# Mixture-of-experts stage of a two-block model: experts in fixed order, rows of each split by bits into 128-, 64- and 32-row blocks

## Chip, cores and metric

The kernel runs on one core of a Trainium2 chip. The metric is the device time of one execution in microseconds (us). Everything is float32. The names of the engines are PE (TensorE), DVE (VectorE), ACT (ScalarE), POOL (GpSimd) and SP (SyncE, which only queues DMAs here).

## What is computed

Two transformer-like blocks over 1,024 tokens of width 1,024. The change lies in the feed-forward part of the first, a mixture of 32 experts: a token picks one of 4 groups, and in it the two best of 8 experts. Cut to that:

```python
p_group, g_idx = lax.top_k(group_probs, 1)
p_exp, e_local = lax.top_k(jax.nn.softmax(e_logits, axis=-1), TOP_K)      # TOP_K = 2, 8 experts of the group
gate = p_group * p_exp / jnp.sum(p_exp, axis=-1, keepdims=True)
flat_e = (g_idx * EXPERTS_PER_GROUP + e_local).reshape(-1)                # 2,048 pairs of token and expert
order = jnp.argsort(flat_e); tok = order // TOP_K
xs = xf[tok]                                                              # rows of 1,024
hid = silu(ragged_dot(xs, w1, group_sizes)) * ragged_dot(xs, w3, group_sizes)   # w1, w3: 1024 x 512 each
ys = ragged_dot(hid, w2, group_sizes) * gate[...]                         # w2: 512 x 1024
```

The sizes of the groups are known only on the chip; the instructions are fixed before. For the inputs used here the router sends to experts 0 to 31, in this order, 84, 29, 15, 50, 38, 32, 32, 28, 126, 111, 72, 24, 72, 92, 57, 100, 54, 96, 89, 14, 25, 23, 37, 18, 132, 213, 64, 47, 28, 40, 63 and 143 rows.

## The kernel before

The program is written out by hand, engine by engine, with semaphores. The stages follow one another: first projections, retention, a delta rule, the residual (which writes the normalised rows `xn_rows`), `route` (the router), `experts_pass`, then `mix` (which gathers each token's two result rows from `y_rows`) and the second block.

**Router.** `route_tensor` (L2095) and `route_vector` (L2140) find each token's experts, its rank among the rows of the expert, and from that its place in `y_rows`. `route_blocks_vector` (L2223) turns the 32 counts into a list of blocks: an expert's rows fill blocks of 128 as long as more than 64 are left; what is then left, 64 at most, is a half block. It writes to the table `experts` which expert each block has, how many blocks of each kind are used, and whether a block's expert differs from that of the block before. `route_places_vector` (L2276) makes the places, 16 small matmuls (L2121) the tokens of each block (`tokens`).

**Experts.** `experts_units` (L2323) fixes an order of 47 units, of which the used ones run: a full block (one expert, 128 rows), or a pair of half blocks (two experts, 64 rows each). Here 13 full blocks and 11 pairs are used, so 24 units run. In `experts_tensor` (L2561), `work` does on PE for a unit: 32 matmuls of 256 columns for w1 and w3, with the transposed rows `e_xsT` as the stationary operand, transposes of the gated result `e_hid` and of the next unit's rows, and 8 matmuls of 512 columns with w2. For a pair, `experts_matmul` (L2551) issues each of these twice, into two column halves of the array. The helpers of ACT (L2645) and DVE (L2696) do silu, gate, copies and the affine step on the way out of the transposes. Every unit ends with one store of 128 rows to `y_rows` from ACT's queue (L2670).

**Control.** Each engine reads three numbers from `experts` into registers (`used_blocks`, L2384) and then meets two branches at a unit (`experts_blocks`, L2535), which always lead straight on as long as units are used; after the last one it jumps over the rest.

**Weights.** An expert's three matrices are 6.3 MB. There are three sets of buffers. The first load is that of expert 0 from a fixed address, queued at the end of the residual (L2354). All others (`experts_load`, L2439) wait until the router's table is there, read the expert's number into a register, and load from an address made of it; a load is left out if the set already holds the expert. That makes 34 loads of an expert here: 12 for full blocks and 22 for half blocks. POOL gathers the rows of each unit six units ahead (L2493).

Of the kernel before, what the change touches and what calls it, by code (L numbers as in the profile page):

```python
# [10 lines left out]
F32 = mybir.dt.float32  # L11
# [23 lines left out]
FULLS = 2 * T // (P // 2 + 1)  # L35
BLOCKS = FULLS + NE // 2
# [1123 lines left out]
def delta_conv_signals(k):  # L1160

    return k.on(CONV_SIGNALS, "w_0 w_1 w_ab_loaded taps_loaded a_log_loaded dt_loaded dn_norm_loaded bias_got bias_stored rpb_spread y_cleared", way="_conv")
# [25 lines left out]
def delta_conv(k, s, b, hT, dtok, z, d, rpb_rows, bias_rows, zero, y_rows, ahead):  # L1188

    cleared = y_rows.rearrange("(p b) (n r c) -> n p (b r) c", p=P, n=CLEARINGS, c=P)  # L1190
# [3 lines left out]
    for p in range(1, CONV_PAIRS):  # L1194
        if p >= 2:
            k.nc.sync.wait_ge(*s.w_summed(4 * (p - 1)))
            k.nc.sync.wait_ge(*conv_made(s, p - 2, 6))
            for role in range(4):
                k.nc.sync.wait_ge(*channels_got(s, p - 2))
                channels_load(k, s, b, p, role)  # L1200
        for n in {1: (0,), CONV_PAIRS - 1: (7,)}.get(p, (2 * p - 3, 2 * p - 2)):
            k.nc.sync.dma_start(cleared[n], wide(zero[:, :], 1, BLOCKS * D // P // CLEARINGS)).then_inc(*s.y_cleared.up().inc)
# [3 lines left out]
    k.nc.sync.wait_ge(*s.y_cleared(CLEARINGS))  # L1206
# [680 lines left out]
def residual_signals(k):  # L1887

    return k.on("out_made rows_gated x_added squared eps_added rstd xn_ready turned_0 turned_1 half_0_out half_1_out",
                "w_got_0 w_got_1 x_got_0 x_got_1 x_got_2 x_got_3 x_stored xn_stored_0 xn_stored_1 first_set_got", way="_res")  # L1890
# [11 lines left out]
def residual(k, s, b, retT, deltaT, hT, affine, x_out, xn_out, route_s, route_w, sets):  # L1902

    residual_sync(k, s, b, x_out, xn_out, route_s, route_w, sets)
# [8 lines left out]
def residual_kept(s):  # L1913

    return s.x_stored, s.xn_stored_0, s.xn_stored_1, s.first_set_got


def residual_sync(k, s, b, x_out, xn_out, route_s, route_w, sets):

    sy = k.nc.sync  # L1920
    for n, got in enumerate((s.x_got_0, s.x_got_1, s.x_got_2, s.x_got_3)):
        for m in (2 * n, 2 * n + 1):
            sy.dma_start(b.x[m][:, :], k.io["x"][m * P:(m + 1) * P, :]).then_inc(*got.up().inc)
    route_load(k, route_s, route_w)
# [5 lines left out]
    for j in range(3):  # L1930
        experts_first_load(k, s, sets, j)
# [96 lines left out]
Route = namedtuple("Route", "wr br lg eq gp top ix ixf sel hot both a1 a2 a3 earlier cnt low left upto0 upto1 first lines whole blk ef place w2 row_of blk_of parts hp hb pos lT fresh below")  # L2028
# [7 lines left out]
def route_loads(k):  # L2036

    return k.on("", "w_group_loaded w_expert_loaded b_group_loaded b_expert_loaded", way="_route"), \
        RouteWeights(k.at("route_w", front_at(82), P, NK, NL), k.at("route_b", front_at(84), P, NL))
# [11 lines left out]
def route(k, loads, weights, h2T, gates, where, tokens, experts):  # L2051


    early, late, wait = packed(k, "route", N_AT), packed(k, "route", N_AT + 144 * KB), packed(k, "route", A_AT)
    b = Route(weights.w, weights.b, early("logits", NT, NL), early("eq", NT, NE), early("gp", NT, 8), early("top", NT, 8), early("ix", NT, 8, dt=U32),
              early("ixf", NT, 8), early("sel", NT, PER_GROUP), late("hot", 2, NT, NE), early("both", NT, NE), late("a1", NT), late("a2", NT), late("a3", NT),
              early("earlier", NT + 1, NE), early("cnt", NE, NT), early("low", NE), early("left", NE), early("upto0", 2, NE + 16), early("upto1", 2, NE + 16),
              late("first", 2, NE), late("lines", 2, NE), late("whole", NE), early("blk", FULLS + NE, NE), early("ef", FULLS + NE), late("place", NT, NE),
              late("w2", NT, NE), late("row_of", NT, 2), late("blk_of", NT, 2), late("parts", 2, NT, 2, dt=U32), wait("hp", NT, 2, P), wait("hb", NT, 2, BLOCKS),
              late("pos", NT, 2), early("lT", BANK), early("fresh", SAME - 1), late("below", NT))  # L2060
    s = k.on("columns_made columns_out logits_made group_shifted group_exp ratio_ready ratio_exp chosen_ready ranks_made counts_ready counts_laid places_ready places_read")
# [33 lines left out]
def route_tensor(k, s, b, h2T):  # L2095
# [17 lines left out]
    keep_warm(k, 4, 7)  # L2113
    pe.wait_ge(*s.counts_ready(1))
    pe.matmul(k.bank[5][:, 0:FULLS + NE], k.c("ones"), b.ef[:, :], start=True, stop=True).then_inc(*s.counts_laid.up().inc)
    keep_warm(k, 7, 7)
    for n in range(NT):
        for j in range(2):
            if n % 4 == j == 0:
                pe.wait_ge(*s.places_ready(n // 4 + 1))  # L2120
            t = pe.matmul(k.bank[3][:, 0:BLOCKS], b.hp[:, n, j, :], b.hb[:, n, j, :], start=n + j == 0, stop=n + j == NT)  # L2121
# [18 lines left out]
def route_vector(k, s, loads, b, gates, where, tokens, experts):  # L2140
# [3 lines left out]
    v.tensor_scalar(b.below[:, :], k.c("token"), -float(NO_TOKEN), None, ALU.add).then_inc(*V.up().inc)  # L2144
    route_groups_vector(k, s, loads, b)
# [18 lines left out]
    v.wait_ge(*s.ratio_exp(1))  # L2164
    v.scalar_tensor_tensor(a3, a2, 1.0, a1, ALU.add, ALU.mult).then_inc(*V.up().inc)
    v.wait_ge(*V.now())
    v.reciprocal(gates[:, :, 0:1].squeeze(2), a3).then_inc(*V.up().inc)
    v.wait_ge(*V.now())
    v.tensor_tensor(gates[:, :, 1:2].squeeze(2), gates[:, :, 0:1].squeeze(2), a2, ALU.mult).then_inc(*V.up().inc)
# [9 lines left out]
    known = route_blocks_vector(k, s, b, experts)  # L2179
# [1907 lines left out]
```

## Time and profile before

| | |
|---|---|
| median of 3 runs | 3054.93 us |
| lowest and highest | 3054.62 and 3062.04 us |
| span of the profiled execution | 3061.1 us |
| own time of the profiled execution | not listed; the highest of the three runs is 0.9 us above the span |
| PE busy | 94% of the span |
| experts' stage, first to last matmul | 953.9 to 1516.8 us of the span |

The profile's page lists busy time of each engine and the costliest groups of instructions; the trace behind it can be asked for stretches, for one engine's instructions in order of time, and for the DMA queues. "Issue" names idle time in which an engine waited for nothing that the trace shows; a wait for a DMA's semaphore that stands in a separate instruction is such a case. A matmul of f32 is recorded as two passes, and a weight load (PEld) before each.

### The profile page before, as it was taken

The page shows a single profiled execution, that of the slowest core. Times are in us where ns is not written, and L with a number is a line of the kernel's source. Part 1 is how long each engine was busy: PE and PEld are TensorE (multiplying, and loading weights), DVE is VectorE, ACT ScalarE, POOL GpSimd, SP SyncE. Part 2 cuts the span into 40 slices and gives each one's busy share as a digit, 9 for nine tenths or more (in the row PEclk, how much of TensorE's full clock was granted, in tenths as well). Part 3 has the DMA queues.
Part 4 walks back from the last instruction along what each step waited for, and adds up shares of the span by engine and source line. Part 5 has one row for each costly group of instructions (what it writes and reads, how often), then busy time and mean ns, then how long its engine had stood idle before and what let it go on. Part 6 is the DMA issues. An engine that isn't in the chain of part 4 may idle for free.

```text
span 3061.1 us, 30798 instructions
## 1 busy us (share of the span) xinstructions
PE 2887.6 (94%) x12002; PEld 1715.2 (56%) x12002; DVE 1208.1 (39%) x1999; ACT 629.8 (21%) x1351; POOL 724.5 (24%) x552
## 2 busy tenths in 40 slices
PE   7999998888988999899889999999999999999998
PEld 5886544888446666566534455557544444444443
DVE  6714776565132111111143135479643314133142
ACT  4001232232121222212222211147230000000001
POOL 3213466543111000000021000146521122111220
PEclk9999999999998999999989999999999999999999
DMA  8734495000237999999661100030201101111101
GB/s 264 224 54 49 99 221 142 1 29 29 112 138 285 396 425 427 425 426 394 252 226 55 55 0 15 14 107 1 90 28 55 55 28 41 41 55 46 37 28 55
DMA packets 180120, 415.12 MB, mean 136 GB/s; under 512 B 30644, under 2 KB 103796, under 8 KB 170872
## 3 DMA queue, kind: packets, MB, share of 16 engines
q1 hardware_dynamic: 163545, 370.52, 34.2%
q10 hardware_dynamic: 10512, 25.69, 2.6%
q0 software_dynamic: 5904, 16.78, 1.5%
q8 instruction: 100, 1.64, 0.2%
q14 instruction: 59, 0.48, 0.0%
HBM read 372.33 MB, written 59.88 MB: 141 GB/s over the span
## 4 chain that ended last, share of the span: by engine, by line
PE 86%; DVE 6%; DMA 3%; issue 2%; ACT 1%; POOL 1%; SPq 0%; ACTq 0%; POOLq 0%; DVEq 0%
PE bank L3791 27%; PE bank L2554 9%; PE bank L2557 8%; PE bank L2984 5%; PE bank L1266 4%; PE bank L748 4%; PE bank L1946 4%; PE bank L3158 3%; PE bank L232 3%; PE bank L3156 2%; PE bank L3490 2%; PE bank L883 2%; PE bank L3500 2%; PE bank L1844 1%; DMA wa_rest<-in_w_ada 1%
## 5 line engine op out<-in xcount | busy, mean ns | idle before, releaser
L3791 PE MATMUL bank<-w_ff,uT 128*128 128x512 f32 x640 | 276.0, 592 | 0.0
L3791 PE MATMUL bank<-hT,w_ff 128*128 128x512 f32 x512 | 224.3, 596 | 4.3 <-DVE hT L3594 4.3
L3914 DVE TENSOR_TENSOR x_out<-x_out,bank 128x512 f32<-128x512 f32 x140 | 94.5, 685 | 291.8 <-PE bank L3791 291.6
L3791 PEld LDWEIGHTS bank<-w_ff,uT 128*128 128x128 f32 x640 | 121.6, 190 | 153.1 <-issue 153.1
L2554 PE MATMUL bank<-e_w,e_xsT 128*128 128x256 f32 x832 | 186.0, 385 | 1.6 <-DVE e_xsT L2640 1.6
L2554 PEld LDWEIGHTS bank<-e_w,e_xsT 128*128 128x128 f32 x832 | 159.3, 193 | 33.0 <-issue 11.3
L2557 PE MATMUL bank<-e_w,e_xsT 128*64 128x256 f32 x1408 | 155.9, 380 | 22.3 <-issue 22.3
L2984 PE MATMUL bank<-w_gla,nT 128*128 128x512 f32 x384 | 168.3, 598 | 2.0 <-ACT nT L2946 1.3
L3791 PEld LDWEIGHTS bank<-hT,w_ff 128*128 128x128 f32 x512 | 97.5, 191 | 126.3 <-issue 126.1
L3791 PE MATMUL bank<-h_sum,w_ff 128*128 128x512 f32 x384 | 166.1, 592 | 0.0
L2711 DVE TENSOR_TENSOR e_hid<-e_act,bank 128x256 f32<-128x256 f32 x48 | 20.2, 422 | 338.4 <-PE bank L2554 172.1
L2557 PEld LDWEIGHTS bank<-e_w,e_xsT 128*64 128x64 f32 x1408 | 111.6, 137 | 70.4 <-issue 33.9
L3855 POOL TENSOR_TENSOR w_ff<-w_ff,w_ff 128x2048 f32<-128x2048 f32 x9 | 42.7, 4746 | 355.8 <-PE bank L3791 352.5
L2984 PEld LDWEIGHTS bank<-w_gla,nT 128*128 128x128 f32 x384 | 73.2, 192 | 92.5 <-issue 89.1
L3828 ACT ACTIVATE uT<-bank 128x512 f32<-128x512 f32 x48 | 28.3, 600 | 468.9 <-PE bank L3791 468.9
L3791 PEld LDWEIGHTS bank<-h_sum,w_ff 128*128 128x128 f32 x384 | 73.0, 190 | 91.8 <-issue 91.8
L3901 DVE TENSOR_TENSOR uT<-uT,bank 128x512 f32<-128x512 f32 x48 | 32.9, 686 | 229.2 <-PE bank L3791 229.2
L3158 PE MATMUL bank<-nT,w_nqk 128*128 128x512 f32 x256 | 121.7, 605 | 0.0
L2493 POOL DMA_INDIRECT e_rows<-xn_rows,e_idx x25 | 25.0, 1001 | 407.8 <-PE bank L2523 379.8
L748 PE MATMUL bank<-w_in,hT 128*128 128x256 f32 x512 | 116.9, 387 | 3.0 <-DVE qkvg L516 3.0
L3475 POOL TENSOR_SCALAR n_sc<-n_sc,n_st 128x512 f32<-128x512 f32 x64 | 99.7, 1563 | 46.9 <-DVE n_st L3458 44.7
L3791 PE MATMUL bank<-w_ff,u_sum 128*128 128x512 f32 x256 | 110.5, 592 | 0.0
(534 smaller groups left out, 4924.0 us busy)
## 6 DMA issues: line engine op xcount, KB each, us to landing
e_w<-in_w SPq DMA_DIRECT2D x108, 2048.0 KB, 21.7
w_ff<-in_w_ff SPq DMA_DIRECT2D x32, 1024.0 KB, 5.3
y_rows<-zero SPq DMA_DIRECT2D x8, 3008.0 KB, 20.4
wa_rest<-in_w_ada SPq DMA_DIRECT2D x32, 512.0 KB, 6.0
y_rows<-e_y ACTq DMA_DIRECT2D x24, 512.0 KB, 9.2
wa<-in_w_ada SPq DMA_DIRECT2D x16, 512.0 KB, 10.7
w_qkv<-in_w_in SPq DMA_DIRECT2D x24, 256.0 KB
w_gla<-in_w_in SPq DMA_DIRECT2D x3, 2048.0 KB, 21.2
```

The costliest lines, as they stand in the source:

```text
L232: t = k.nc.tensor.transpose(bank[:, h * P:(h + 1) * P], src[:, h * P:(h + 1) * P], k.c("ident"))
L748: t = pe.matmul(out, still[:, f, g * P:(g + 1) * P], moving[:, f, :], start=step in (0, 1, 3) and g % 2 == f == 0, stop=f == 3, skip_group ...
L883: t = pe.matmul(k.bank[6 + m % 2][:, :], hT[:, f, m * P:(m + 1) * P], wz[:, f, :], start=f == 0, stop=f == NK - 1)
L1266: t = pe.matmul(conv_bank(k, p, step)[:, :], weights[step][:, f, :], tokens[step](f), start=step in (0, 1, 3) and f == 0, stop=f == 3, ski ...
L1946: t = pe.matmul(k.bank[2 * (m % 2) + h][:, :], mixed, b.w[h][:, f, :], start=f == 0, stop=f == NK - 1)
L2554: return pe.matmul(out, xT, weights[0], start=start, stop=stop)
L2557: t = pe.matmul(out[tokens, :], xT[:, tokens], w, start=start, stop=stop)
L2984: t = pe.matmul(k.bank[3 * (i % 2) + j][:, :], b.nT[:, f, i * P:(i + 1) * P], b.w[at][:, f, :], start=f == 0, stop=f == NK - 1)
L3158: t = pe.matmul(bank[:, :], wqk[c // 2 % 2][:, f, c % 2 * P:(c % 2 + 1) * P], nT[:, f, h * BANK:(h + 1) * BANK], start=f == 0, stop=f == N ...
L3475: g.tensor_scalar(b.sc[n][:, :], b.sc[n][:, :], b.st[n][:, 2:3], None, ALU.mult).then_inc(*s.weights_ready.up().inc)
L3791: t = pe.matmul(bank[:, :], still, moving, start=step in (0, 1, 3) and f == 0, stop=f == 3, skip_group_check=True)
L3914: v.tensor_tensor(dst, dst, k.bank[4 * ((ph + step) % 2) + g][:, :], ALU.add).then_inc(*s.added.up().inc)
```

## The change

The experts are taken in the order 0 to 31. Each is loaded once, from fixed addresses, in that order and into three sets of buffers in turn, so that the SP queue needs nothing from the router. An expert's rows, rounded up to 32, are split by bits: 128 or more give a block of 128 (what is above 255 goes to 14 spare blocks at the end, none used here), bit 64 a block of 64, bit 32 a block of 32. By the counts above this makes six blocks of 128 (experts 8, 9, 15, 24, 25, 31), sixteen of 64 and twenty of 32. Experts 8, 9 and 15 have nothing but the block of 128; nine experts have only the 64, eleven only the 32; seven have both (0, 10, 12, 13, 17, 18, 25), and 24 and 31 have 128 and 32.

For each expert every engine reads the row count of the next from the table and branches on its bits. PE has five arms for each expert, of which it jumps over what is not needed. A 64-row block uses both column halves of the array for the two halves of w1 (then w3); a 32-row block uses four column quarters for the halves of w1 and w3 together. The 128-row block has the weights as stationary operand and 128 token columns moving, so that its result needs no transposes. `y_rows` has 78 x 128 rows now instead of 47 x 128, and eight of sixteen clearing DMAs come after the store of `bias_rows`.

The core of the diff, in the order of the program:

```diff
@@ delta_conv (SP queue) @@
-    k.nc.sync.wait_ge(*s.y_cleared(CLEARINGS))
+    for n in range(CLEARINGS, 2 * CLEARINGS):
+        k.nc.sync.dma_start(cleared[n // CLEARINGS, n % CLEARINGS], wide(zero[:, :], 1, GATHERS // 2)).then_inc(*y_cleared.up().inc)
@@ experts (SP queue) @@
+def experts_load(k, s, b, e):
+    sy, n = k.nc.sync, e % SETS
+    for j, ((dst, src), got) in enumerate(zip(experts_weights(k, b, slice(e, e + 1), n), experts_loaded(s))):
+        if e >= SETS:
+            if j == 0:
+                sy.wait_ge(*s.turned_0(e - SETS + 2))
+                sy.wait_ge(*s.turned_1(e - SETS + 2))
+            elif j == 2:
+                sy.wait_ge(*s.down_made(2 * (e - SETS + 1)))
+            sy.wait_ge(*got[n](e // SETS))
+        sy.dma_start(dst[:, :, :], src).then_inc(*got[n].up().inc)
+def experts_first_loads(k, s, b, xn_stored):
...
+    for e in range(SETS):
+        experts_load(k, s, b, e)
@@ PE @@
+def quarter_up_tensor(k, s, b, e, n, made):
+    for i in range(NK):
+        for h in range(4):
+            w = (b.w1[n], b.w3[n])[h // 2]
+            t = pe.matmul(k.bank[6][h * QUARTER:(h + 1) * QUARTER, 0:2 * P], b.x[:, i, HALF:TAIL], w[:, i, h % 2 * 2 * P:(h % 2 + 1) * 2 * P], start=i == 0, stop=i == NK - 1)
+def experts_tensor(k, s, f, b, experts):
...
+    for e in range(NE):
+        n = e % SETS
+        following = experts_rows_of(pe, experts, e + 1) if e + 1 < NE else None
+        pe.wait_ge(*up[n](e // SETS + 1))
+        pe.wait_ge(*gate[n](e // SETS + 1))
+        with pe.If(rows >= P):
+            pe.wait_ge(*down[n](e // SETS + 1))
+            full_tensor(k, f, b, e, n)
+        with pe.Else():
+            full_skipped_tensor(k, f)
+        if e + 1 < NE:
+            full_turn_next(k, s, f, b, e + 1, following)
+        pe.wait_ge(*s.x_out_a(4 * (e + 1)))
+        pe.wait_ge(*s.x_out_v(4 * (e + 1)))
+        with pe.If((rows & HALF) > 0):
+            with pe.If((rows & QUARTER) > 0):
+                half_up_tensor(k, s, b, e, n, 1)
+                quarter_up_tensor(k, s, b, e, n, 1)
+                tail_turn_next(k, s, f, b, e)
...
+        with pe.Else():
+            with pe.If((rows & QUARTER) > 0):
+                quarter_up_tensor(k, s, b, e, n, 3)
+                tail_turn_next(k, s, f, b, e)
+                pe.wait_ge(*s.hid_ready(2 * e + 2))
+                quarter_turn_tensor(k, s, b, 2)
+                pe.wait_ge(*down[n](e // SETS + 1))
...
+                pe.wait_ge(*s.hidT_out(2 * e + 2))
+                quarter_down_tensor(k, s, b, n, 2)
@@ ACT and DVE, an expert with 32 rows alone @@
+                a.wait_ge(*s.up_made(3 * e + 3))
+                silu(b.act_q[HALF:P, :], k.bank[6][0:HALF, 0:2 * P], 2)
+                tail_next_scalar(k, s, b, e, scale, shift)
+                quarter_store(k, s, b, e, ys, 2)
...
+                gated(b.act_q[HALF:P, :], k.bank[6][HALF:P, 0:2 * P], 2)
+                tail_next_vector(k, s, b, e, scale, shift)
+                v.wait_ge(*s.hid_turned(2 * e + 2))
+                turned(b.hidT_q[:, :], k.bank[6][:, 0:P], 2)
```

How it moves the instructions, at two places. On PE, a unit before (a full block; `e_rows` are the next unit's rows, `e_hid` the gated result):

```order
L2540 COMPARE_AND_BRANCH
L2542 COMPARE_AND_BRANCH
L2554 MATMUL bank<-e_w_2_1_5786,e_xsT_1_6680 128x256 x8
L2554 MATMUL bank<-e_w_2_1_5787,e_xsT_1_6680 128x256 x8
L2554 MATMUL bank<-e_w_2_1_5786,e_xsT_1_6680 128x256 x8
L2554 MATMUL bank<-e_w_2_1_5787,e_xsT_1_6680 128x256 x8
L2593 MATMUL bank<-consts_49,e_hid_6683 128x128 x2
L2523 MATMUL bank<-consts_49,e_rows_1_6674 128x128 x8
L2593 MATMUL bank<-consts_49,e_hid_6683 128x128 x2
L2554 MATMUL bank<-e_w_2_1_5788,e_hidT_6684 128x512 x8
L2542 UNCONDITIONAL_BRANCH
```

and, of the change, the end of expert 0's arm for 32 rows alone, its arm for none, and the head of expert 1:

```order
L2579 MATMUL bank<-e_w_2_1_6340,e_xT_6354 32x256 x2
L2520 MATMUL bank<-consts_49,e_rows_1_6349 128x96 x8
L2593 MATMUL bank<-consts_49,e_act_q_6357 128x64 x2
L2613 MATMUL bank<-e_w_2_1_6341,e_hidT_q_6360 32x256 x16
L2695 UNCONDITIONAL_BRANCH
L2520 MATMUL bank<-consts_49,e_rows_1_6349 128x96 x8
L2705 UNCONDITIONAL_BRANCH
L2423 TENSOR_LOAD experts_57
L2423 ISA x2
L2663 COMPARE_AND_BRANCH
```

Between one expert's matmuls and the next one's a register load and branches now stand, and the transposes of `e_act_q` follow the whole of the up-projection instead of lying between two parts of it. On ACT, a full unit before (silu, copy of the transposed result, next rows, result) is

```order
L2660 ACT_TABLE_LOAD
L2660 ACTIVATE e_act_6682<-bank 128x256 x2
L2663 ACTIVATE e_hidT_6684<-bank 128x256 x2
L2642 ACTIVATE e_xsT_1_6681<-bank,affine_rows_58 128x128 x4
L2667 ACTIVATE e_y_1_6685<-bank 128x512
L2670 DMA y_rows<-e_y_1_6685 128x1024
```

and expert 0's arm for 32 rows alone, with the head of its arm for none, is now

```order
L2807 ACT_TABLE_LOAD
L2807 ACTIVATE e_act_q_6357<-bank 64x256
L2729 ACTIVATE e_xT_6354<-bank,affine_rows_58 128x96 x4
L2788 ACTIVATE e_y_q_6362<-bank 128x256
L2790 DMA y_rows<-e_y_q_6362 4x32x256
L2834 UNCONDITIONAL_BRANCH
L2729 ACT_TABLE_LOAD
L2729 ACTIVATE e_xT_6354<-bank,affine_rows_58 128x96 x4
```

The copy of the transposed result has moved from ACT to DVE, and the arm without a 64 or 32 block (last two rows) has a table load of its own ahead of the next rows.

## Rows read from the trace of the kernel before

**Rows 1.** Page, the chain that ended last, by engine.
```profile
PE 86%; DVE 6%; DMA 3%; issue 2%; ACT 1%; POOL 1%; SPq 0%; ACTq 0%; POOLq 0%; DVEq 0%
```
**Rows 2.** The experts' stretch: length; busy of PE, PEld, DVE, ACT, POOL; clock, DMA share, GB/s.
```profile
953.90:1516.90 563.00, 540.59 (x3088) 365.65 (x3088) 69.00 (x168) 114.12 (x240) 18.02 (x19) 0.99 0.93 387
```
**Rows 3.** PE in that stretch by form: busy, mean ns, idle before.
```profile
L2554 PE MATMUL bank<-e_w,e_xsT 128*128 128x256 f32 x832 | 186.0, 385 | 1.6 <-DVE e_xsT L2640 1.6
L2557 PE MATMUL bank<-e_w,e_xsT 128*64 128x256 f32 x1408 | 155.9, 380 | 22.3 <-issue 22.3
L2554 PE MATMUL bank<-e_w,e_hidT 128*128 128x512 f32 x208 | 91.4, 592 | 0.0
L2557 PE MATMUL bank<-e_w,e_hidT 128*64 128x512 f32 x352 | 78.0, 595 | 0.0
L2523 PE MATMUL bank<-consts,e_rows 128*128 128x128 f32 x192 | 25.3, 275 | 0.0
```
**Rows 4.** PE in order of time: start, length, idle before.
```profile
950.37 1.97 PE L2523 MATMUL bank<-consts,e_rows 128*128 128x128 f32 x8 [4.66 <-DMA e_rows<-xn_rows,e_idx]
953.89 17.11 PE L2554 MATMUL bank<-e_w,e_xsT 128*128 128x256 f32 x64 [1.55 <-DVE e_xsT L2640]
...
1232.02 3.67 PE L2557 MATMUL bank<-e_w,e_xsT 128*64 128x256 f32 x32 [1.64 <-issue]
...
1281.50 3.67 PE L2557 MATMUL bank<-e_w,e_xsT 128*64 128x256 f32 x32 [1.71 <-issue]
```
**Rows 5.** A window inside the stretch, columns as in rows 2.
```profile
1250.00:1300.00 50.00, 46.44 (x276) 31.48 (x276) 6.89 (x18) 10.49 (x23) 2.00 (x3) 1.00 1.01 426
```
**Rows 6.** PE elsewhere, small shapes, by form (columns as in rows 3).
```profile
L1246 PE MATMUL bank<-nT,w_z 128*32 128x512 f32 x32 | 7.1, 594 | 0.0
L2091 PE MATMUL bank<-hT,route_w 128*36 128x128 f32 x32 | 1.9, 274 | 1.5 <-DVEq L164 1.5
...
L3371 PE MATMUL bank<-qkvr,g_AT 128*128 128x128 f32 x96 | 13.9, 288 | 0.0
```
**Rows 7.** ACT and DVE in the experts' stretch, by form.
```profile
L2660 ACT ACT_TABLE_LOAD x24 | 30.8, 1283 | 77.7 <-PE bank L2557 42.9 <-PE bank L2554 33.8 <-DVE e_y L2717 0.8
L2660 ACT ACTIVATE e_act<-bank 128x256 f32<-128x256 f32 x48 | 18.4, 384 | 149.5 <-PE bank L2554 77.3 <-PE bank L2557 72.0
L2640 DVE TENSOR_SCALAR e_xsT<-bank,affine_rows 128x128 f32<-128x128 f32 x96 | 32.8, 405 | 16.8 <-PE bank L2523 16.8
L2711 DVE TENSOR_TENSOR e_hid<-e_act,bank 128x256 f32<-128x256 f32 x48 | 20.2, 422 | 338.4 <-PE bank L2554 172.1 <-PE bank L2557 166.3
```
**Rows 8.** Router's table done, and SP's first weight DMA that reads it, in order of time.
```profile
922.24 0.19 DVE L2272 CAST experts<-route_ef 128x63 int32<-128x63 f32 x1
...
925.55 0.11 SPq L2458 DMA_DIRECT2D e_w<-in_w  x1
```
**Rows 9.** DMA queue q8 in 0 to 900, 1550 to 3061, 1510 to 1514, 1514 to 1518: packets, MB, share.
```profile
q8 instruction: 33, 0.54, 0.3%
...
q8 instruction: 38, 0.62, 0.2%
...
q8 instruction: 1, 0.02, 1.5%
...
q8 instruction: 1, 0.02, 2.1%
```
**Rows 10.** End of the experts' stage, in order of time.
```profile
1516.83 0.60 ACT L2667 ACTIVATE e_y<-bank 128x512 f32<-128x512 f32 x1 [5.09 <-PE bank L2554]
...
1517.61 0.33 ACTq L2670 DMA_DIRECT2D y_rows<-e_y  x1
1521.90 0.34 SPq L2775 DMA_DIRECT2D x_tile<-x_rows  x1
```
**Rows 11.** A window with gaps on PE: length, busy, clock, DMA share, GB/s.
```profile
1229.00:1233.00 4.00, 2.36 (x14) 1.00 1.00 422
```
**Rows 12.** The delta stage's first window, columns as in rows 2.
```profile
520.00:540.00 20.00, 11.15 (x51) 9.55 (x52) 9.74 (x16) 6.30 (x10) 11.05 (x11) 0.67 0.00 0
```

More of the change, by code:

```diff
@@ L2022, in residual_scalar @@
                 a.activation(hT[:, f, (m - 1) * P:m * P], src, ACT.Identity, scale=affine[:, 2, f:f + 1], bias=affine[:, 3, f:f + 1]).then_inc(*s.half_0_out.up().inc)
-Route = namedtuple("Route", "wr br lg eq gp top ix ixf sel hot both a1 a2 a3 earlier cnt low left upto0 upto1 first lines whole blk ef place w2 row_of blk_of parts hp hb pos lT fresh below")
+Route = namedtuple("Route", "wr br lg eq gp top ix ixf sel hot both a1 a2 a3 earlier rounded bits full half spare upto0 upto1 extra shift own over rest offs place w2 far "
+                   "row_of blk_of parts hp hb pos lT below ends cmp ids")
 NL = GROUPS + NE
@@ L2051, in route @@
 def route(k, loads, weights, h2T, gates, where, tokens, experts):
[L2054 to L2060, printed above, removed]
@@ L2112, in route_tensor @@
     pe.matmul(k.bank[2][:, 0:NE], k.c("ones"), b.earlier[:, NT, :], start=True, stop=True).then_inc(*s.ranks_made.up().inc)
[L2113 to L2116, printed above, removed]
+    keep_warm(k, 11, 7)
     for n in range(NT):
@@ L2518, in experts_turn @@
-def experts_turn(k, s, b, at, half):
-    out = (s.half_0_turned, s.half_1_turned)[half]
-    for q in range(4):
-        f = half * 4 + q
-        t = k.nc.tensor.transpose(k.bank[half][:, q * P:(q + 1) * P], b.rows[at % ROWS_AHEAD][:, f:f + D - NK + 1:NK], k.c("ident"))
-    t.then_inc(*out.up().inc)
-HALF = DE // 2
-def experts_up_bank(k, part, j):
-    return k.bank[((2, 3), (7, 4))[part][j]][:, 0:HALF]
-def experts_blocks(engine, used, work, skip, rest, at=0):
-    if at == BLOCKS:
-        return
-    end = min(at + 2, BLOCKS)
-    with engine.If(group_used(used, at)):
-        for u in range(at, end):
-            with engine.If(unit_used(used, UNITS[u])):
-                work(u)
-            with engine.Else():
-                skip(u)
-        experts_blocks(engine, used, work, skip, rest, end)
-    with engine.Else():
-        rest(at, BLOCKS - at)
@@ new lines, in full_skipped_tensor, with half_up_tensor @@
+def full_skipped_tensor(k, f):
+    pe = k.nc.tensor
+    pe.sem_inc(*add(f.up_made, 2))
+    pe.sem_inc(*add(f.down_made))
+def half_up_tensor(k, s, b, e, n, last):
+    pe = k.nc.tensor
+    for j, w in enumerate((b.w1[n], b.w3[n])):
+        if j:
+            pe.wait_ge(*s.y_out(2 * e)) if e else None
+        for i in range(NK):
+            for h in range(2):
+                t = pe.matmul(k.bank[2 + j][h * HALF:(h + 1) * HALF, 0:2 * P], b.x[:, i, 0:HALF], w[:, i, h * 2 * P:(h + 1) * 2 * P], start=i == 0, stop=i == NK - 1)
+        t.then_inc(*add(s.up_made, last if j else 1))
```

857 lines of the change are left out of this document (490 added, 367 removed).

## The prediction

> **What bounds the kernel now.** I read the chain of waits first: PE carries 86% of it, DMA 3% [rows 1]. The change touches the experts' stage and little else, so the second view is that stretch: 563.0 us from its first to its last matmul, PE busy for 540.6 of them and the DMA engines busy for 0.93 [rows 2]. Both are near their limit there, and the question is which one waits. The rows by form answer it: PE's idle time is 22.3 us ahead of the pairs' matmuls and 1.6 at the start [rows 3]. In order of time they are waits such as 1.64 and 1.71 us ahead of a pair's first matmuls [rows 4], in windows in which the DMA engines are at 1.01 and 426 GB/s [rows 5]: PE waits there for a load. So the stage is 24 units of PE work at 22.4 us (540.6 / 24 = 22.5), with short load waits from its middle on. What the change does to PE's time per expert decides; fewer bytes can give back 22.3 us at most.
>
> **PE's matmuls.** Per pass, from rows 3: 256 columns against the full array 0.220 us (186.0 less about 3 for the slow first unit, over 832), two half-array passes side by side 0.2215 (155.9 / 1408, twice), the same of 512 columns 0.443, a full pass of 512 columns 0.439, a transpose 0.13.
> - A 64-row block takes 32 slots of 0.2215 and 8 of 0.443: 10.6 us. Sixteen: 170 us. That is just what half of a pair costs today.
> - A 32-row block takes 16 + 8 slots of four passes each. The trace has no four side by side; its 128*32 row runs two at a time (7.1 us for 32 passes of 512 columns, 0.222 each, half of 0.443) [rows 6]. If four overlap, a slot is 0.2215; if only two do, 0.443. Issue also counts: 32 weight loads and passes took 1.9 us, 0.06 a pair, so four pairs need 0.24 [rows 6]. I take 0.24: 5.8 us a block, twenty blocks 115 us; bounds 106 and 213.
> - A 128-row block takes 128 passes of 128 columns, each with its own weight load. Half of 0.220 is the lower bound, 0.145 (13.9 / 96, [rows 6]) the upper. I take 0.117, near the lower one, because weight loads of the same size hide in the full blocks of rows 3: 15.0, and 16 x 0.439 = 7.0 for w2: 22.0 us. Six: 132 us; bounds 127 and 154.
> - Transposes: 31 groups for 64/32 rows and six for 128 rows at 1.0, and 36 short pairs at 0.25: 46 us.
>
> Together 463 us, where 540.6 stand now. The rounding to 32 does save 78 us of array time.
>
> **What PE now waits for inside an expert.** Before, the gate of the first half ran under the second half's matmuls, and the transposes of the next rows under the rest, so PE had no gap. Now the up-projection of a tail ends as one piece. For a 32-row block alone ACT then loads its table (1.28) and does the silu (0.38), DVE the gate (0.42) [rows 7], and DVE, in its order, the affine step of the next expert's rows (four of 0.34, a little less for 96 columns: 1.3) before the copy of the transposed result (0.3). With hand-overs that is 3.9 us; PE has 1.2 us of transposes in it, so 2.7 idle, for 13 experts (11 alone, 2 behind a 128 block): 35 us. For a 64-row block alone silu and table load hide under w3: 2.9 less 1.2 = 1.7, nine times: 15. With both, 1.5, seven times: 10. After a 128 block without a tail ACT copies and stores the result (0.6 + 0.33 [rows 10]), loads a table again (1.28) and then writes the next rows (1.4, taken from DVE's 4 x 0.34), for which PE stands: 4 us, three times: 12. Sum 72 us, which nothing hides, since the next expert's matmuls are queued behind.
>
> **What PE waits for between experts.** Before, branches always went straight on and PE's queue covered them. Now PE reads the next count into a register. From the router's table to SP's first dependent DMA 3.1 us pass, with four such reads [rows 8]: 0.75 each. With the branches and waits, 1.1 us. A 64 block leaves 3.5 us of matmuls queued over that, so it costs nothing; a 32 block hardly any, since issuing its 64 loads and passes takes as long as running them. I count 0.8 for 19 such changes (15 us) and 4 us for the three 128-row experts.
> The jumps are the second part. Counted in the built programs, PE has 1,131 instructions per expert (128 rows 290, both tails 380, 64 alone 184, 32 alone 216), of which a 32-row expert runs a quarter. Queue q8 carries PE's instructions: packets of 16 KB, 33 in the first 900 us and 38 after 1550, where the program has 8,627 instructions up to the experts (a few hundred of them after 900) and 9,743 behind them, so 256 a packet [rows 9]. At the end of the stage PE jumps over some 7,600 instructions, and just there two packets come within 8 us; the skipped ones never do [rows 9]. So PE keeps little more than the page it is in and the next, and a jump beyond must fetch. The 2.1% share of 16 engines in 4 us is 1.3 us of transfer [rows 9]; from the last store to SP's next DMA, a stretch that holds such jumps, a drain and the release, 4.0 us pass [rows 10]. Zero and 4.0 are the bounds; I take 2.5, twice the transfer. A 32-alone expert has one sure miss (564 instructions skipped), a 64-alone one about half, leaving the arm for both two thirds. Not covered by queued work: 8 x 2.5 + 5 x 1.25 + 7 x 1.65 = 38 us. Control together: 57 us.
> The Trainium skill (Runtime: NRT & Kernel Launch, "Instruction fetch mechanics") says that a taken branch to outside the fetched window stalls for a DMA, which is what rows 9 show. The same section gives PE room for 2,048 instructions; by that no jump here would leave it, which is a rival below.
>
> **The rest.** SP queues three sets before the router is done. The gathers of the first rows then no longer compete with loads for long, and the block table's chain is shorter, while 78 instead of 47 columns are compared: I let the first up-projection start at 950 instead of 953.9 [rows 4], and it is slow by the same 3 us. Loads: from one such pair to the next, with a full unit between, three experts are loaded in 49.5 us [rows 4], 16.5 each with rows and stores; 29 after about 965 end near 1443, long before PE gets to the last expert, so the two loads saved buy only the 22.3 us. The extra clearing (8 DMAs) falls into the delta stage, whose DMA share is 0.00 [rows 12], and costs nothing; if that cover were gone, x and router weights would be late. POOL's 64 gathers run experts ahead and are not waited for. At the end ACT must see its stores land and read one more register: +1.5 us.
>
> **Sum.** 463 + 72 + 57 + 3 = 595 us from 950: end at 1545, where it was 1516.8 [rows 10]. That is 28 us more, with the exit 30. On the profiled span of 3061.1 us this makes 3091; that execution stands 6 us above the median of 3054.93, so the forecast is **3084 us**.
>
> **Rivals.**
> 1. *Jumps and issue cost nothing* (the other side). If PE holds the arms ahead, as the page's 2,048 instructions would have it, the 38 us go; with slots at their lower bounds (449) the loads then bind a little (8 us): 449 + 72 + 19 + 3 + 8 = 551, end 1501, and 1.5 for the exit: **3041 us**. It decides where a miss costs under about 0.6 us together with full overlap. For it: branches never cost PE anything in this trace. Against it: they all led straight on but the last, and that one fetched. Chance 0.25.
> 2. *Four quarter-array passes run two at a time*: +98 us, **3182 us**. For it: two is all that the trace shows. Against it: half-array passes overlap fully. Chance 0.08. The Trainium skill (TensorE: Matmul & The Clock Gate, "Packing small matmuls") measured 3.07 times for four tiles; by that a slot would be 0.29, the sum 24 us more. No run here shows it yet.
> 3. *The clock.* A 32-row expert keeps PE busy for 7 of 12 us. The granted clock fell to half after idle stretches such as that ahead of the first unit, which took 17.11 instead of 14 us [rows 4]; but in a window with PE busy for 2.36 of 4 us it stayed at 1.00, the 2.4 GHz level [rows 11]. If half of the 11 such experts run at 1.2 GHz: +32 us, **3116 us**. Chance 0.14.
> The forecast itself has 0.53.
>
> **Numbers.** The three runs lie within 0.24%, so 0.3% (9 us) is about what a measurement can tell from no change. The forecast's own range is 3060 to 3115 (a miss at 1.5 or 3.5 us, slots at their bounds). Including rival 1 down to 3032 and rival 3 up to 3145 leaves out rival 2 and the ends. Faster than 3046: most of rival 1, 0.22. Within 9 us: its rest and the forecast's low end, 0.15. Slower: 0.63.
>
> **What would show it.** Right: from first to last up or down matmul of the experts about 595 us, though PE is busy for only some 460 to 470; idle of some 2.7 us ahead of the 32-row down matmuls, released by DVE's copy; 3 to 4 us ahead of a 32-alone up-projection; some 90 q8 packets or more within the stage; a DMA share well under 0.93; 5.8 us for a 32-row block. Wrong: PE idle ending with loads, q8 packets at a steady rate with no gap beside them, 32-row slots at 0.44 us, or a clock under 0.95.

## The result, and the profile after

The changed kernel takes **3401.91 us** (median of 4, 3392.54 to 3409.85) where the kernel before takes 3058.48: a ratio of 1.1127, 95% interval 1.111 to 1.1144. The forecast was 3084 us with a range from 3032 to 3145: the sign was right, the size far off, 318 us too small. The profiled execution took 3409.85 us, its span 3408.0.

From the page of the changed kernel: PE's row, the row of granted clocks, the instruction queue, and the chain of waits by engine (to be read against [rows 1]).

```profile
PE 2879.5 (84%) x13346; PEld 1681.4 (49%) x13346; DVE 1223.6 (36%) x2063; ACT 661.8 (19%) x1393; POOL 758.1 (22%) x591
PEclk9999997999976787876978899999999999999999
q8 instruction: 208, 3.41, 0.4%
PE 75%; issue 10%; DVE 6%; DMA 3%; SPq 2%; ACT 2%; POOL 1%; DVEq 0%; ACTq 0%; POOLq 0%
```

"Issue" now has 10% of the chain: PE waits for nothing that the profile can name. The experts' stage by itself, from the first up-projection to the end of the last 128-row block (a 32-row block of 9 us follows), as a window: length, busy times, granted clock, DMA share, GB/s. [Rows 2] is its counterpart.

```profile
972.73:1857.00 884.27, 530.92 (x4334) 332.71 (x4334) 78.71 (x235) 144.26 (x278) 56.54 (x58) 0.78 0.59 229
```

PE's waits in that window: total, times, longest.

```profile
PE bank L2569 <- issue: 137.8, 16, 17.6
PE bank L2579 <- issue: 134.8, 12, 15.7
PE bank L2520 <- issue: 22.5, 6, 8.9
PE bank L2603 <- DVE e_hidT_h L2898: 22.4, 16, 1.5
PE bank L2593 <- DVE e_act_q L2897: 15.7, 12, 1.3
PE bank L2613 <- DVE e_hidT_q L2898: 14.6, 12, 1.2
PE bank L2520 <- ACT e_xT_f L2729: 3.7, 1, 3.7
...
PE bank L2543 <- issue: 1.8, 1, 1.8
```

So 884 us are 531 of PE work, 297 of "issue" (137.8 + 134.8 + 22.5 + 1.8) and 56 behind DVE and ACT. Of the "issue" time 272.6 us stand ahead of up-projections, in 28 pieces of which three are the second part of a split gap: 10.9 us for each of 25 tails (272.6 / 25). Experts 24, 25 and 31, whose tail comes behind a 128-row block of their own, have no gap there. One in order of time (start, length, idle time ahead in brackets):

```profile
1045.95 2.80 PE L2613 MATMUL bank<-e_w,e_hidT_q 128*32 128x256 f32 x32 [1.22 <-DVE e_hidT_q L2898]
1048.87 0.38 ACT L2788 ACTIVATE e_y_q<-bank 128x256 f32<-128x256 f32 x1 [3.64 <-PE bank L2613]
...
1054.28 1.01 POOL L2462 DMA_INDIRECT e_rows_f<-xn_rows,e_idx  x1 [21.61 <-PEq L2644]
```

PE's 32-row block ends at 1048.75. POOL's gather is released at 1054.28 by L2644, the signal that PE's sequencer gives on its way past the 128-row arm. The next up-projection starts at 1059.97, after 11.23 us. Half of the gap lies before that signal and half behind it, and in 1050 to 1058 three 16 KB packets of q8 arrive. In the whole execution q8 has 208 packets, where the kernel before has 100.

Behind the stage nothing changed: 1541.7 us are left after it (3408.0 - 1866.3) and 1544.2 before (3061.1 - 1516.9). The rest of the loss comes earlier. Of PE's waits in the first 711 us the longest is new:

```profile
PE bank L230 <- SPq L162: 27.8, 1, 27.8
```

Line 162 is the meeting of all engines. SP comes to it late, behind the eight further clearings. The windows show what stands there (520 to 545, to be compared with [rows 12]):

```profile
520.00:545.00 25.00, 0.49 (x4) 0.25 (x3) 1.82 (x5) 3.26 (x5) 4.06 (x4) 0.52 1.15 348
```

PE is busy for 0.49 of 25 us, the DMA share is 1.15. The stage starts at 972.73 instead of 953.89 [rows 4].

### The profile page after: what moved, and what is told of

It is laid out like the page before. It is cut to its first block, busy times and chain, and to the rows that moved or that the text cites. A ratio compares the mean times of both kernels' runs of the same rounds, so it can differ in the third digit from the quotient of the medians.

```text
span 3408.0 us, 34547 instructions
## 1 busy us (share of the span) xinstructions
PE 2879.5 (84%) x13346; PEld 1681.4 (49%) x13346; DVE 1223.6 (36%) x2063; ACT 661.8 (19%) x1393; POOL 758.1 (22%) x591
## 4 chain that ended last, share of the span: by engine, by line
PE 75%; issue 10%; DVE 6%; DMA 3%; SPq 2%; ACT 2%; POOL 1%; DVEq 0%; ACTq 0%; POOLq 0%
PE bank L4005 25%; PE bank L2569 4%; PE bank L3198 4%; PE bank L746 3%; PE bank L1944 3%; PE bank L3372 3%; PE bank L2579 3%; PE bank L2543 3%; PE bank L1265 3%; PE bank L230 3%; PE bank L2603 2%; PE bank L3370 2%; PE bank L3704 2%; PE bank L881 2%; PE bank L3714 2%
## 5 line engine op out<-in xcount | busy, mean ns | idle before, releaser
L2569 PE MATMUL bank<-e_w,e_xT 128*64 128x256 f32 x1024 | 149.1, 460 | 139.8 <-issue 137.8
L2579 PE MATMUL bank<-e_w,e_xT 128*32 128x256 f32 x1280 | 98.2, 470 | 134.9 <-issue 134.8
L2462 POOL DMA_INDIRECT e_rows_f<-xn_rows,e_idx x32 | 32.8, 1024 | 740.7 <-PEq L2644 506.8
L2569 PEld LDWEIGHTS bank<-e_w,e_xT 128*64 128x64 f32 x1024 | 90.9, 168 | 200.0 <-issue 176.4
L2579 PEld LDWEIGHTS bank<-e_w,e_xT 128*32 128x32 f32 x1280 | 49.0, 134 | 184.6 <-issue 169.9
L2897 DVE TENSOR_TENSOR e_act_q<-e_act_q,bank 64x256 f32<-64x256 f32 x20 | 8.5, 425 | 286.4 <-ACT e_act_q L2807 286.4
```

The lines of the kernel that those rows point to most:

```text
L2569: t = pe.matmul(k.bank[2 + j][h * HALF:(h + 1) * HALF, 0:2 * P], b.x[:, i, 0:HALF], w[:, i, h * 2 * P:(h + 1) * 2 * P], start=i == 0, stop ...
L2579: t = pe.matmul(k.bank[6][h * QUARTER:(h + 1) * QUARTER, 0:2 * P], b.x[:, i, HALF:TAIL], w[:, i, h % 2 * 2 * P:(h % 2 + 1) * 2 * P], start ...
```

## Experiments

Two theories stood against each other at first. **Fetch**: the gaps are instruction pages that PE must fetch after it has jumped over code. **Branch**: reading the count, deciding and signalling cost it, whatever the distance. Behind them, **loads**: a wait for weights that the rows don't name. Each run was timed beside the kernel before (3057 to 3060 us); "less" and "more" are against the 3401.91 us of the changed kernel where nothing else is named. The runs e2, e3 and e4 have two executions each, the others four or more.

### Arms that are not taken, emptied on PE (e1)

`ROWS_NOW` holds the counts of this input plus 31; `h` and `q` are its bits of 64 and 32.

```diff
         with pe.If(rows >= P):
-            pe.wait_ge(*down[n](e // SETS + 1))
-            full_tensor(k, f, b, e, n)
+            if ROWS_NOW[e] >= P:
+                pe.wait_ge(*down[n](e // SETS + 1))
+                full_tensor(k, f, b, e, n)
...
             with pe.If((rows & QUARTER) > 0):
+                if h and q:
...
```

> PE's branches and register reads stay, but the arms that this input never takes are empty on PE, so a jump skips nearly nothing. Every matmul, load and gather that was executed stays. Theory fetch (the 12 us ahead of each tail's up-projection are instruction pages that PE must fetch after jumping over code): those gaps shrink from 12 us to 1 us or less, q8 falls from 208 packets to about 110, the granted clock in the stage returns from 0.78 to over 0.95, the stage goes from 892 us to 530 to 570, the whole to about 3060 us. Theory branch (reading the register, deciding and releasing cost it, whatever the distance): gaps stay at 10 to 12 us, 3380 to 3400 us. Theory loads (PE waits for weights in a way that the waits don't name): gaps stay too, with less than 20 us gained.

Measured: 3242.61 us (3235.96 to 3250.17), 159 less. q8 fell to 111 packets. The gaps marked "issue" fell to 20 us in all (the two rows below and 5.7 elsewhere), mostly 1.2 to 1.5 us ahead of an up-projection: branches and reads are all still there, so theory branch holds for that much only. But the total fell by half of what was expected, and the clock only rose to 0.85. PE's waits in the stage:

```profile
PE bank L2523 <- ACTq L2771: 74.5, 8, 21.0
PE bank L2572 <- ACT e_y_q L2798: 35.6, 3, 18.8
PE bank L2606 <- DVE e_hidT_h L2908: 21.0, 16, 1.5
...
PE bank L2572 <- ACT e_y_h L2787: 12.4, 1, 12.4
PE bank L2523 <- ACT e_xT_f L2739: 11.9, 2, 6.5
PE bank L2572 <- issue: 8.3, 5, 3.3
PE bank L2582 <- issue: 6.1, 5, 1.5
```

A second wait stood behind the first. In order of time:

```profile
1009.01 32.90 SPq L2392 DMA_DIRECT2D e_w<-in_w  x5
...
1036.23 0.38 ACT L2798 ACTIVATE e_y_q<-bank 128x256 f32<-128x256 f32 x1 [25.17 <-DMA y_rows<-e_y_q]
...
1039.52 1.52 PE L2523 MATMUL bank<-consts,e_rows 96*128 96x96 f32 x8 [20.95 <-ACTq L2771]
```

ACT can't copy a result while the store of the one before, issued at 1002.92, is still under way 33 us later; it writes the next rows behind that, and PE stands. The packets of ACT's queue (q10) in 8 us of that time (1017 to 1025), with those of the weights' queue (q1):

```profile
q1 hardware_dynamic: 308, 2.98, 92.6%
...
q10 hardware_dynamic: 25, 0.05, 1.7%
```

### Only one of the two jumps (e2, e3)

The same edit for the 128-row arm alone, and for the tail arms alone.

> As the run before it, but only the 128-row arm (and the transposes for it) is empty where not taken; the three tail arms stay, so one of the two jumps per expert (over some 290 instructions) goes and the other (over 216 to 564) stays. Theory fetch: each gap loses 4 to 6 of its 12 us, the total falls by 120 to 190 us to about 3250 us. If a single fetch at the end of both jumps were what costs: under 60 us. Theories branch and loads: no change, 3400 us.

> The mirror of the run before it: the tail arms that are not taken are empty on PE, the 128-row arm stays and is jumped over 26 times. Theory fetch: gaps lose the other half, 3220 to 3280 us; the two halves together give what emptying both gives. If only the long jumps over the tail arms miss: all is gained here, about 3060 us, and nothing in the run before. Theories branch and loads: 3400 us.

Measured: 3300.92 us (101 less) and 3274.06 (128 less). The "issue" gaps: 192 us with the tails' jumps alone (102.8 + 76.1 + 12.7), 140 with the 128-row arm's alone (75.7 + 51.3 + 12.9); together 332, against 295 in the same three lines with both. So each jump has its own price and neither is hidden under the other. The totals add up to 229, more than the 159 of emptying both, since from there on the stores bind.

### The same jumps without the loads (e4)

```diff
+        if e >= SETS:
+            sy.sem_inc(*got[n].up().inc)
+            continue
         sy.dma_start(dst[:, :, :], src).then_inc(*got[n].up().inc)
```

> The changed kernel with all its jumps, but SP signals the weights of experts 3 to 31 as there without loading them, so that the queues are nearly idle in the stage (those experts compute with the first three sets of weights). Theory fetch with contention (a page waits behind 6 MB of weights in the same 16 engines): gaps shrink from 12 to 4 to 7 us, total about 3200 us. Theory fetch without contention (a page has its own latency): gaps stay at 11 to 12 us, 3390 us. Theory loads: gaps go to 1 us, about 3060 us. Theory branch: 3390 us.

Measured: 3276.16 us, 126 less, with a DMA share of 0.09 in the stage.

```profile
PE bank L2582 <- issue: 77.6, 11, 10.9
PE bank L2572 <- issue: 77.2, 15, 11.8
...
PE bank L2523 <- issue: 17.0, 6, 4.6
```

That is 174 us with one more of 1.8, where 297 stood. The gaps ahead of up-projections are 6.0 us each (154.8 / 26), as fetch with contention had it (4 to 7); the total is 76 us above that theory's 3200. Loads are not what PE waits for: without them most of the gap time remains, and in e1, where all loads stand and PE asks for them sooner, only 20 us are left. So the other 123 us are what the loads' traffic adds to the jumps: it makes them 1.7 times as dear.

### Plain stores (e5, e9)

```diff
-    a.dma_start(ys[e * P + HALF:e * P + TAIL, :].rearrange("r (h c) -> h r c", h=4), b.y_q[:, :]).then_inc(*add(s.q_stored))
+    for h in range(4):
+        a.dma_start(ys[e * P + HALF:e * P + TAIL, h * 2 * P:(h + 1) * 2 * P], b.y_q[h * QUARTER:(h + 1) * QUARTER, :]).then_inc(*add(s.q_stored))
```

The 64-row store likewise in two, and the waits on their signals scaled.

> As e1_untaken_empty, but each tail's rows are stored with plain two-dimensional transfers, two of 64 x 512 for a 64-row block and four of 32 x 256 for a 32-row block, instead of one transfer whose outer dimension is 2 or 4. In e1 a store of 128 packets still had packets moving 30 us after its issue, and ACT waited 178 us for such stores before it could copy the next result. Theory narrow (the transfer with an outer dimension of 2 or 4 is served by few of the 16 engines): the stores land in 9 us or so, ACT's waits for them fall to below 20 us, and of e1's 3243 us some 120 to 150 go: about 3110 us. Theory buffer (any store lands late behind the weights, one buffer per block size is what is short): waits stay, 3230 us.

Measured: **3116.13 us** (3108.76 to 3120.27), 126 less than with the arms emptied alone. The stores' queue moved 259 packets in 4 us (1000 to 1004), where it had moved 25 in 8, and PE's waits for ACT fell from 134 us (the four rows of e1) to 10. The stage:

```profile
973.95:1572.90 598.95, 503.55 (x4434) 322.74 (x4434) 80.24 (x238) 146.51 (x281) 56.49 (x58) 0.91 0.85 336
```

599 us. The forecast's sum without its 38 us for fetches is 557; of the 42 more, 38 are the matmuls at a clock of 0.91 (503.6 for 463 + 3). The Trainium skill (DMA: Bandwidth & Descriptors, "Why a DMA increments its semaphore by 16 and not by 1") says that the number of engines that share a transfer is the largest k up to 16 that divides the slowest dimension of both access patterns. By that the changed kernel's stores went to 2 and 4 engines, the plain ones to 16; the packet rates agree, though no run here counted the engines.

The same edit in the changed kernel itself:

> The changed kernel with plain stores and nothing else. In e1 and e5 plain stores gave 126 us once the jumps were gone. In the changed kernel no row shows ACT waiting for a store: 12 us of jump stand ahead of each up-projection and the late stores land behind them. Theory cover: less than 20 us gained, 3385 to 3405 us. If the slow stores also delay something else (pages in the same engines, since their packets hold those engines for 30 us): 30 us or more.

Measured: 3408.52 us (3400.21 to 3415.86), no gain. In the changed kernel the jumps hide the stores completely.

### Clearings behind the meeting (e6)

```diff
-    for n in range(CLEARINGS, 2 * CLEARINGS):
-        k.nc.sync.dma_start(cleared[n // CLEARINGS, n % CLEARINGS], wide(zero[:, :], 1, GATHERS // 2)).then_inc(*y_cleared.up().inc)
...
     k.meet()
+    for n in range(CLEARINGS, 2 * CLEARINGS):
+        k.nc.sync.dma_start(cleared[n // CLEARINGS, n % CLEARINGS], wide(zero[:, :], 1, GATHERS // 2)).then_inc(*y_cleared.up().inc)
```

> The changed kernel with the second eight clearings issued behind the meeting of the engines that ends the convolution, and nothing else. In the changed kernel PE waits 27.8 us at that meeting for SP, whose queue takes a clearing every 7.3 us; the kernel before had no such wait. Theory meeting: the wait goes, and 19 to 28 us with it: 3374 to 3383 us. Theory contention (the clearings' own traffic slows the delta stage wherever they stand): less than 10 us gained, above 3392 us.

Measured: 3377.07 us (3370.91 to 3377.65), 24.8 less. The first up-projection starts at 946.65. The clearings' traffic, 0.87 of the DMA engines in 520 to 545, costs the delta stage nothing; only their place ahead of a meeting did.

### What control and distance cost (e7, e11, e12)

Plain stores, and on PE `if rows >= P:` over the counts of this input in place of each branch (e7):

> As e5_plain_stores, but PE has neither register reads nor branches for the experts: the arms that this input takes follow one another. ACT and DVE keep theirs. It prices read and branch by themselves: in e1 1.2 to 1.5 us ahead of each up-projection. Theory control: 31 times 1.0 to 1.3 us, 30 to 40 us less than e5. If that time only covered another wait (a load, ACT): less than 15 us.

Measured: 3102.89 us (3101.60 to 3103.69), 13 less. With PE free of branches, "issue" still shows 15.4 us, most of it ahead of 128-row blocks, which need all three weights: PE had caught up with the loads. Reads and branches cost 13 us here, the rest covered that wait.

Jumps over code that never runs, put back into that version (e11):

```diff
+        if e % 4:
+            with pe.If(never > 0):
+                for _ in range((0, 16, 72, 141)[e % 4]):
+                    pe.matmul(k.bank[2][:, 0:2 * P], b.x_f[:, 0, :], b.w1[n][:, 0, 0:2 * P], start=True, stop=True)
         pe.wait_ge(*up[n](e // SETS + 1))
```

> e7 (PE without branches) with a jump put back ahead of 24 of the 31 later experts, over code that never runs: 64 instructions ahead of experts 1, 5, 9, ..., 288 ahead of 2, 6, ..., 564 ahead of 3, 7, ..., none ahead of 4, 8, ... Theory page: over 64 instructions the gap is 1 to 2 us or now and then one fetch, over 288 always one fetch, 4 to 6 us, over 564 one too, since skipped pages are not fetched: 4 to 6 us as well; total 3103 + 8 x (1 + 5 + 5) = 3190 us. If the cost grows with distance (all skipped pages are fetched): 2, 5 and 10 us, 3240 us. If branches do not cost (the gap of the changed kernel is something else): 3115 us.

Measured: 3168.17 us (3167.36 to 3171.86), 65 more; q8 rose from 109 to 135 packets. Four experts in a row, with 564, 0, 64 and 288 instructions ahead of them:

```profile
1348.41 6.48 PE L2582 MATMUL bank<-e_w,e_xT 128*32 128x256 f32 x64 [5.21 <-issue]
...
1362.20 4.74 PE L2582 MATMUL bank<-e_w,e_xT 128*32 128x256 f32 x64
...
1374.44 3.77 PE L2582 MATMUL bank<-e_w,e_xT 128*32 128x256 f32 x64
...
1390.85 9.22 PE L2572 MATMUL bank<-e_w,e_xT 128*64 128x256 f32 x64 [3.73 <-issue]
```

The eight jumps over 64 instructions left at most 1.3 us. Over 288 the gap was 0 to 4.4 us. Over 564 it was 4.7 to 8.1 us for six (some split in two, the second part inside the block) and 0.5 and 1.2 for the two that lead to a 128-row block behind a 64-row one. So the page theory was wrong for 288, which costs a fetch only now and then; whether 564 costs more for its length or for nearly always missing this run doesn't tell. Nor does it tell why the 128-row arm of about the same length (290) costs 4.8 us a gap in e3: that difference stays open.

And in the kernel before (e12):

```diff
     def work(at):
...
+        with pe.If(used[0] > NE):
+            for _ in range(141):
+                pe.matmul(k.bank[2][:, 0:HALF], b.xsT[n][:, 0, :], b.w1[sets[0]][:, 0, 0:HALF], start=True, stop=True)
```

> The kernel before with one jump over 564 instructions that never run, put at the start of each unit of PE, where 7 us of down-projection matmuls are queued. Theory cover (a page fetch costs only what outlasts the queued matmuls; in the changed kernel the jumps behind a 128-row arm showed no gap): under 1 us a unit, 3057 to 3075 us. If a jump costs its 5 us wherever it stands: 24 x 5 = 120 us, 3175 us.

Measured: 3059.47 us, ratio 1.0000 (0.9989 to 1.0011). This says nothing about a jump, because the edit put none into the program. `used_blocks` reads `used[0]` with a stated maximum of `NE`:

```python
    return [engine.value_load(experts[0:1, at + n:at + n + 1], min_val=0, max_val=(NE, NE, 2 * NE)[n]) for n in range(3)]
```

So `used[0] > NE` can never hold, and the built program has neither the comparison nor the 564 instructions. The instruction queue agrees. It has the same line as in the kernel before, where the 24 jumps of e11 brought 26 packets more:

```profile
q8 instruction: 100, 1.64, 0.2%
```

Whether queued work covers a jump can be read in the changed kernel itself, at two places only. Experts 24 and 31 have 128 and 32 rows: from the 128-row arm PE jumps over the two arms with 64 rows (564 instructions) to the one for 32 rows alone.

```profile
1641.61 7.03 PE L2550 MATMUL bank<-e_w,e_act_f 128*128 128x512 f32 x16
1648.47 1.04 PE L2520 MATMUL bank<-consts,e_rows_f 128*128 128x128 f32 x8
1649.44 3.66 PE L2579 MATMUL bank<-e_w,e_xT 128*32 128x256 f32 x64
...
1850.47 7.03 PE L2550 MATMUL bank<-e_w,e_act_f 128*128 128x512 f32 x16
1857.44 3.66 PE L2579 MATMUL bank<-e_w,e_xT 128*32 128x256 f32 x64
```

There is no gap ahead of either up-projection, with 7.03 us of w2 matmuls queued at the jump; e4, e6 and e9 show none at these two places either. No run varies the queued work alone, so how much is enough is not shown.

### Two attempts at a better kernel (e8, e10)

The first works for any routing. PE's three tail arms become pieces with a branch each, the up-projections ahead of the 128-row arm; plain stores; clearings behind the meeting.

```diff
-        with pe.If((rows & HALF) > 0):
-            with pe.If((rows & QUARTER) > 0):
...
+        with pe.If(half):
+            half_up_tensor(k, s, b, e, n, 1)
+        with pe.Else():
+            pe.sem_inc(*add(s.up_made, 2))
+        with pe.If(quarter):
+            quarter_up_tensor(k, s, b, e, n, 1)
...
+        with pe.If(rows >= P):
...
```

> A kernel that works for any routing: clearings behind the meeting, plain stores, and PE's three tail arms (380, 184 and 216 instructions) replaced by four short pieces behind a branch of their own (64-row up, 32-row up, 64-row down, 32-row down), the up-projections ahead of the 128-row arm, so that the jump over it and over the other piece comes while matmuls are queued. Code per expert falls from 1,131 to about 730 instructions. Theory fetch: fewer and shorter jumps and some cover: q8 from 208 to about 150 packets, gaps per expert from 12 to 4 to 7 us, in all 3180 to 3260 us. If every jump out of the current page costs its full 5 us wherever it stands, there are three now instead of two: no better than 3380 us.

Measured: 3238.33 us (3231.06 to 3244.93), 139 less than with the clearings alone (e6), for the pieces and the plain stores together. q8 has 165 packets; what is left is the jump over the 128-row arm:

```profile
PE bank L2520 <- issue: 119.0, 28, 6.6
```

28 times 4.3 us, though the up-projection of 3.7 us or more is issued ahead of it. It seems that a queue of short matmuls covers less than one of long ones; no run tests that by itself.

The second is for this input alone: e7's edit on ACT and DVE too, the clearings behind the meeting, and in DVE's arms:

```diff
-                tail_next_vector(k, s, b, e, scale, shift)
                 v.wait_ge(*s.hid_turned(2 * e + 2))
                 turned(b.hidT_q[:, :], k.bank[6][:, 0:P], 2)
+                tail_next_vector(k, s, b, e, scale, shift)
```

> A version for this input alone, to see what the blocks are worth without control: clearings behind the meeting, plain stores, no register reads or branches for the experts on PE, ACT and DVE, and DVE copies the transposed result before it writes the next expert's rows instead of behind them. From e7's 3103: 24 for the clearings, 25 to 30 for DVE's order (29 waits of 1.2 to 1.5 us for its copy), and up to 20 if ACT's table load ahead of each silu goes with its branches: 3030 to 3055 us, against 3057 before. If loads bind from here on (29 x 16.5 us from 965 end at 1443, the stage at about 1500): not under 3045.

Measured: 3064.01 us (3059.51 to 3070.86), ratio 1.0018 (1.0007 to 1.0030): no better than the kernel before, and 9 us above the top of what was expected. DVE's order did its part (its copies are waited for 15.7 us, where it was 37.0 in e7), but waits of 11.3 and 11.2 us stand ahead of 128-row blocks, in windows such as this one (PE busy 0, DMA share 1.03):

```profile
1346.40:1357.50 11.10, 0.00 (x0) 0.00 (x0) 0.00 (x0) 0.39 (x1) 0.00 (x0) 0.67 1.03 378
```

Without control the blocks run into the loads: 573.6 us from first to last, DMA share 0.88. A run of this version without loads was not made. No version here beats the kernel before.

## Why the prediction was wrong, by its steps

The stage took 893.5 us (972.7 to 1866.3), where the sum had 595. Of the 298 more, 240 are control (297 for 57) and 71 the matmuls at the lower clock; the gaps inside an expert, with 2.6 us in the last block, took 13 less. The later start adds 23.

- **Control between experts, 57 us: the step that failed.** It was 297 us, of which at most 20 (the gaps left in e1) are reads and branches, as forecast. The fault is in the fetches, both in their number ("A 32-alone expert has one sure miss") and in their price (2.5 us). In truth most tails have two uncovered jumps, one over other tail arms, at a mean of 5.8 us with its reads and branches (e2, 192 over 33 gaps), and one over the 128-row arm, at 4.8 us (e3, 140 over 29). The 290 instructions of the 128-row arm were not counted as a miss at all. Nor did the 3.5 us of matmuls that a 64-row block leaves queued cover anything to speak of: behind the one of expert 3 the gap was 13.96 us. And the price was sized at "twice the transfer", from a single fetch at the end of the stage [rows 9, 10], while in the stage a page arrives beside weight loads (e4: 174 us without them, 297 with them); the upper bound of 4.0 came from that same quiet place.
- **The clock, 3 us: failed as a consequence.** PE's work took 530.9 us at a granted 0.78, and 5.9 more in the last 32-row block: 537 in all, 71 more than 463 + 3. With the gaps gone the same matmuls, the last block included, took 503.6 (0.91). Rival 3 named this and priced it at 32 for gaps of 5 us; [rows 11] with PE busy for 2.36 of 4 us was too short an idle stretch to judge 12 us by.
- **Start at 950: failed by 22.7 us.** "The extra clearing ... falls into the delta stage ... and costs nothing" overlooked that SP issues them ahead of a meeting of all engines, where its queue took one in 7.3 us. Behind the meeting the start is at 946.65 (e6).
- **The stores: a wait that the sum did not have.** It is hidden in the changed kernel (e9), and worth 126 us once the jumps are gone (e1 and e5). The prediction has stores in the time of a load ("16.5 each with rows and stores") and at the end. That ACT may not copy a result until the store of the one before has landed, in its new shape, it did not price.
- **Array, 463 us: right** at full clock. A 32-row block is 3.66 + 1.93 = 5.6 us (5.8 forecast), a 64-row block 7.1 + 3.65 = 10.8 (10.6), a 128-row block 14.56 + 7.03 = 21.6 (22.0). Rival 2 is out: 64 passes of a quarter take 3.66 us, 0.229 for four, where one half-array pair takes 0.2215 [rows 3]. The Trainium skill (TensorE: Matmul & The Clock Gate, "Packing small matmuls") measured 3.07 times for four tiles packed by rows of the array. Here four are packed by columns, and the measurement is 3.9 times, if one alone takes the 0.2215 of a pair (4 x 0.2215 / 0.229).
- **Gaps inside an expert, 72 us: right in kind, 16 too high.** They were 56 (22.4 + 15.7 + 14.6 + 3.7).
- **Loads not binding: right** for the changed kernel, DMA share 0.59; they would bind at 570 us or so (e7, e10).

How far the rest of the sum holds is shown by e5, with jumps and slow stores gone: 599 us for the stage, 557 by the forecast's other terms, and the clock is nearly all of the difference. The 3116 us of e5, near the 3084 forecast, are no support for it, since it has no fetches to pay. Of the signs listed as "right", four came: DVE's copy ahead of the 32-row down matmuls (1.3 + 1.2 us), 133 q8 packets in the stage (28 before), the DMA share, the 32-row block. Two did not: the stage's length with PE busy for 460 to 470, and the 3 to 4 us ahead of an up-projection. One listed as "wrong" came too, a clock under 0.95. Rival 1 rested on a rule of the Trainium skill (Runtime: NRT & Kernel Launch, "Instruction fetch mechanics") that gives PE room for 2,048 instructions. Six of eight jumps over 564 left 4.7 us or more (e11), so the trace disagrees with that figure. That a branch outside the window stalls for a fetch agrees.

## What to carry to other kernels

Code that a branch skips is not free on the engine that sets the pace: count the instructions between where it leaves and where it lands, ask how much work is queued over that point (behind 7 us of long matmuls two jumps left no gap, behind 2 to 4 us of short ones most did), and price a fetch in the traffic of that stage, not at its quiet end. Ahead of a meeting nothing that fills a queue is free, not even on an engine with nothing else to do. And when a test comes out as "no change", look for a sign in the trace that the edit is there at all, as the unchanged count of q8 packets told of e12. When a wait of 12 us goes, look for what it hid: here one for the stores, 134 us in all, stood behind it.

## What the runs showed of the hardware that was not expected

- An uncovered jump, with its reads and branches, costs PE 4.8 to 5.8 us while loads run (e2, e3), and about 60% of that with idle DMA engines (174 / 297, e4).
- Jumps over 64 instructions left at most 1.3 us, over 288 up to 4.4, over 564 from 0.5 to 8.1 (e11); two over 564 behind 7.03 us of queued matmuls left nothing.
- A store of 128 packets whose outer dimension is 4 was still under way 33 us after its issue beside weight loads; with 64 or 32 rows outermost the stores' queue moved 259 packets in 4 us.
- Four quarter-array passes of 256 columns take 0.229 us together, where two half-array passes take 0.2215.
- Eight clearings of 2.5 MB hold SP for 7.3 us each at a DMA share of 1.15.
- The granted clock followed the gaps: 0.78 over the stage with 297 us of "issue" gaps, 0.91 with 20 (e5).
